# A Trainium2 transformer kernel without its filler products in four norms and the routing

## What is computed

```python
# first block, each layer l
h = rms_norm(x, g_norm_mix[l]) * (1 + sc1) + sh1
x = x + g1 * (concat(attention, hgrn2, gmlp of (h @ w_in[l])) @ w_out[l])
h = rms_norm(x, g_norm_ffn[l]) * (1 + sc2) + sh2
y = swiglu(h, ...)            # layer 0
y = moe_swiglu(h, ...)        # layer 1: 8 experts, the best 2 of each token
x = x + g2 * y
# then a norm by g_final, and the second block, each layer l
h = rms_norm_2(x, ln1_gain[l]);  x = x + concat(three mixers of (h @ w_in[l])) @ w_out[l]
h = rms_norm_2(x, ln2_gain[l]);  x = x + square(relu(h @ w_up[l])) @ w_down[l]
```

## Time and profile before

| | |
|---|---|
| median of 3 runs | 2403.26 us (2402.55 to 2404.16) |
| the profiled execution's own time | 2402.56 us |
| its span, first to last instruction | 2400.6 us |
| mean granted TensorE clock | 0.979 |
| TensorE busy with matmuls | 2308.3 us, 96% of the span |
| VectorE, ScalarE busy | 835.9 us (35%), 386.4 us (16%) |
| DMA | 582.92 MB, mean 243 GB/s |

### The profile page before, as it was taken

The page is one execution under the profiler, slowest core; times in us unless marked ns, Lnnn a source line. Parts: engine busy times, 40 slices in busy tenths (PEclk is TensorE's granted clock), DMA queues, the critical chain, the costliest instruction groups (busy, mean ns, idle before and its releaser), DMA issues.

```text
span 2400.6 us, 35155 instructions
## 1 busy us (share of the span) xinstructions
PE 2308.3 (96%) x15101; PEld 1612.3 (67%) x15102; DVE 835.9 (35%) x2042; ACT 386.4 (16%) x903; POOL 27.9 (1%) x52
## 2 busy tenths in 40 slices
PE   7999999999999999999999999899899999989999
PEld 5768888877764444434443444377589998659999
DVE  3663635048320000000000000144566742557663
ACT  3222100022320000000000000023521002441101
POOL 1010000000000000000000000000000000000000
PEclk9998999999899999999999999999999999999999
DMA  9473586622169999999989999973135463323441
GB/s 362 153 266 130 200 318 253 228 102 106 36 252 381 373 409 411 408 412 408 378 300 375 407 410 411 406 249 122 36 100 162 162 219 100 120 71 104 163 158 50
DMA packets 225518, 582.92 MB, mean 243 GB/s; under 512 B 19898, under 2 KB 79810, under 8 KB 213076
## 3 DMA queue, kind: packets, MB, share of 16 engines
q1 hardware_dynamic: 224788, 580.52, 64.6%
q0 software_dynamic: 576, 0.13, 0.0%
HBM read 579.58 MB, written 1.05 MB: 242 GB/s over the span
## 4 chain that ended last, share of the span: by engine, by line
PE 87%; DMA 4%; DVE 4%; SPq 2%; ACT 2%; issue 1%; DVEq 0%; ACTq 0%
PE wrk L2354 13%; PE acc L862 10%; PE wrk L1592 6%; PE acc L2414 5%; PE acc L3133 5%; PE acc L3165 5%; PE wrk L2339 4%; PE acc L865 4%; PE wrk L3165 4%; PE wrk L3133 4%; DMA ring<-in_moe_w_down_dram 3%; PE acc L1609 3%; PE wrk L2361 3%; PE acc L936 2%; PE acc L2397 2%; PE acc L951 2%
## 5 line engine op out<-in xcount | busy, mean ns | idle before, releaser
L2354 PE MATMUL wrk<-ring,hT 128*64 128x512 f32 (+1 forms) x1792 | 348.4, 542 | 6.6 <-DMA ring<-in_moe_w_up_dram 3.3
L2598 DVE TENSOR_TENSOR scratch<-scratch,wrk 128x512 f32<-128x512 f32 (+4 forms) x32 | 24.6, 768 | 802.5 <-PE wrk L2354 595.5
L862 PE MATMUL acc<-hT,ring 128*128 128x256 f32 (+2 forms) x1152 | 263.3, 385 | 1.3 <-ACT scratch L892 0.5
L2354 PEld LDWEIGHTS wrk<-ring,hT 128*64 128x64 f32 x1792 | 126.2, 137 | 204.1 <-issue 186.9
L862 PEld LDWEIGHTS acc<-hT,ring 128*128 128x128 f32 (+2 forms) x1152 | 211.3, 186 | 42.8 <-issue 4.4
L2414 PE MATMUL acc<-ring,scratch 128*64 128x512 f32 x784 | 177.7, 597 | 14.9 <-DMA ring<-in_moe_w_down_dram 14.9
L3210 DVE TENSOR_TENSOR ring<-ring 128x512 f32<-128x512 f32 (+1 forms) x192 | 155.2, 863 | 1.2
L1592 PE MATMUL wrk<-hT,ring 128*128 128x256 f32 x704 | 154.8, 380 | 0.0
L1592 PEld LDWEIGHTS wrk<-hT,ring 128*128 128x128 f32 x704 | 132.8, 190 | 18.6 <-ACT hT L748 0.9
L2414 PEld LDWEIGHTS acc<-ring,scratch 128*64 128x64 f32 x784 | 54.0, 136 | 116.9 <-issue 102.2
L3165 PE MATMUL acc<-scratch,ring 128*128 128x128 f32 x1024 | 117.6, 275 | 0.0
(11 more groups left out here) (439 smaller groups left out, 2713.2 us busy)
## 6 DMA issues: line engine op xcount, KB each, us to landing
ring<-in_moe_w_gate_dram SPq DMA_DIRECT2D x56, 2048.0 KB, 21.3
ring<-in_moe_w_up_dram SPq DMA_DIRECT2D x56, 2048.0 KB, 20.6
ring<-in_moe_w_down_dram SPq DMA_DIRECT2D x56, 2048.0 KB, 19.9
ring<-in_w_ada_dram SPq DMA_DIRECT2D x24, 2048.0 KB, 14.7
ring<-in_w_up_dram SPq DMA_DIRECT2D x32, 1024.0 KB, 7.4
ring<-in_w_down_dram SPq DMA_DIRECT2D x32, 1024.0 KB, 6.5
ring<-in_w_out_dram SPq DMA_DIRECT2D x8, 2048.0 KB, 8.1
ring<-in_w_in_dram SPq DMA_DIRECT2D x8, 1536.0 KB, 13.7
```

Of the source, the lines that this page charges most:

```text
L862: mm = pe.matmul(acc[p0:p0 + m, bank, 0:S], cols(k), hT[:, k, :], start=(k == 0), stop=(k == KD - 1))
L2354: mm = pe.matmul(flat_wrk[h * HD:h * HD + HD, lo:lo + n2], hT[:, k, 0:HD], w[:, at_, h * n2:(h + 1) * n2], start=(k == 0), stop=(k == KD - ...
```

## The change

The helper `keep_busy_pe` and its three calls go. Nothing else is altered.

```diff
@@ norm_pe
             if tag == ("mix", 1):
                 for i in range(4, 8):
                     ada_pe(pe, 1, i)
-            elif tag != ("mix", 0):
-                keep_busy_pe(pe, 10 if tag[0] == "ffn" else 7)
-
-        def keep_busy_pe(pe, n, bank=acc):
-
-            for _ in range(n):
-                pe.matmul(bank[:, 0, 0:S], ones, K("slot_ids"), start=True, stop=True)
@@ joint_norm_pe
                         mm.then_inc(pe_done, up("pe", "sum of squares", bank))
-            keep_busy_pe(pe, 7)
@@ route_pe
             mm.then_inc(pe_done, up("pe", "h turned"))
-            keep_busy_pe(pe, 6, wrk)
             pe.wait_ge(dve_done, at("dve", "selected"))
```

## The result

The changed kernel took 2421.32 us (median of 6 runs, 2417.67 to 2423.15), the kernel before in the same series 2407.59 us. The ratio is **1.0053**, with a 95% interval of 1.0039 to 1.0068: slower by 0.5%, where 0.5% was forecast. A second series of runs gave 1.0065 (1.0051 to 1.0078). The profiled execution took 2417.67 us, against 2402.56 for that of before. The kernel before itself ran anywhere from 2398 to 2414 us, so two single executions say little; the traces have to be taken apart.

The account below looks back on a forecast made before the run. PE, busy 96% of the span, was taken to bound the kernel. Three norms 4.5 plus routing 7.0 made 11.5 us on 2402.56, or 2414.1; 0.7 more for the median gave about 2415 us, range 2407 to 2421.

Parts of the forecast that it names:

- What bounds the kernel: Whole kernel: PE is busy 96% of the span, so time it loses in dense stretches is kernel time.
- What the removal takes off the path: All five filler places: other engines end the waits, so removal gains 0, at most 1 us.
- Norm 0: Layer 0's feed-forward norm: half clock in the dense products behind it costs 1.5 us, bounds 0 to 2.8.
- The two norms of the second block: First norms of both layers there: half clock in the dense work behind costs 1.5 us each, bounds 0 to 2.8.
- The term of 4.5 us for the three norms: Layer 0's feed-forward norm and the second block's two: 3 x 1.5 = 4.5 us, 0 to 8.4.
- The routing: Layer 1's feed-forward norm through the first gathering: thin work at half clock adds 7.0 us, 1 to 9.5.
- Rounds: Routing's 8 rounds of logits and transposes, 48 instructions: half clock adds 5.0 us.
- The sign that L2310 would start 6 to 7 us later: First gathering in the changed profile: starts 6 to 7 us later, measured from the norm's last square.
- That the rounds restore the clock: Rival in the routing: clock recovers after one low stretch; 7.5 us in all, 2411, chance 0.17.
- That the clock holds everywhere: Rival for all waits: clock never falls, not slower; 2402.3 to 2403.3 us, chance 0.10.
- Low for long: Rival: norms pay 2.5 us each, routing stays low until the experts, 9.5; 17 us, 2420, chance 0.12.
- The Trainium skill's rule on transposes: Routing's rounds: transposes do not count for the clock, so it stays low until the gathering; 14 us, 2417.

Follow-up runs that it names:

- no_layer1: Kernel before with the fillers left out only in layer 1's feed-forward norm and in the routing; ratio 1.0036.
- turns: Kernel before with each 256-column filler product replaced by four transposes of a 128 by 128 matrix; ratio 1.0009.
- no_norms: Kernel before with the fillers left out only in layer 0's feed-forward norm and the second block's two first norms; ratio 1.0021.
- pad26: Changed kernel plus 26 one-column products at the program's start, making its stream ahead of the second block as long as before; ratio 1.0046 to the kernel before.
- no_ffn1: Kernel before without only the ten fillers of layer 1's feed-forward norm, the routing's six kept; one run, 2409.12 us.
- half: Kernel before with about half of the fillers at each place, all at the start of the wait; ratio 1.0054.

## Why the prediction was right, and where not

**What bounds the kernel.** Right. Nothing behind the changed places took a delay up: from the end of the norm 0 column to layer 1's mixing norm 215.8 us passed in all fourteen executions, and the experts took 878 to 880.

**What the removal takes off the path.** Right, nothing: the first product in the norm of layer 0 started 0.16 us sooner after ScalarE's start, and with the clock held (norm 0 of no_layer1 and turns) the distance is 29.13 in either case.

**Norm 0.** 1.5 us forecast, 1.3 to 1.4 measured in all five executions without its fillers.

**The two norms of the second block.** 1.5 each forecast. Behind layer 1's it was 0, 1.7, 2.8 and 2.9 us in four executions, 1.8 on average; what follows the joint norm's wait cost 2.7 and 1.7 in the two profiles of the changed kernel and 2.9 in no_norms and pad26, 2.5 on average. The assumed stretch of 3.4 us was too short for these two: 6.8 us is as common. The term of 4.5 us for the three norms was undersized, at 1.4 + 2.5 + 1.8 = 5.7. The trace of the kernel before could have warned of it. The 4.18 us that the prediction reads the earlier trace rows are the busy part of a low stretch of 6.8 us, and with TensorE busy almost throughout one lasts four times 3.41 us, so that "the other low stretches read here last 3.41 us" comes from having read few (columns as in rows 11):

```profile
34.45:41.27 6.82, 4.17 (x7) 2.36 (x8) 1.75 (x10) 4.80 (x9) 0.00 (x0) 0.50 1.06 373
188.05:201.70 13.65, 12.87 (x132) 10.30 (x131) 6.57 (x13) 3.35 (x6) 0.00 (x0) 0.50 0.09 34
```

**The routing.** 7.0 us forecast, 6.1 measured. Rounds: 5.0 forecast; from the first logits to the counts it is 685.75 - 674.12 = 11.63 instead of 7.55 us, 4.1 more. Counts: 1.0 forecast; a pair every 0.43 instead of 0.22 us, 1.0. Gathering: 1.0 forecast, 6.56 - 5.41 = 1.15. The first term was too large because the first instructions still ran before the clock fell, and because a round then takes 1.17 / 0.62 = 1.9 times as long, not twice. The sign that L2310 would start 6 to 7 us later behind the norm's last square did not come: it is 4.9 us (19.37 against 14.43).

**The rivals.** That the rounds restore the clock is refuted by no_ffn1 (low to their end, 8.91 us) and by the 20.48 us of the changed kernel. That the clock holds everywhere is refuted by norm 0 and the routing of every kernel without fillers there; behind norm 1 it did hold once in four. "Low for long" came partly true for the second block's norms, but the routing never reached its upper bound. The Trainium skill's rule on transposes would have given 2417; turns shows that its reason does not hold in these waits.

**What the prediction did not have.** The sentence "the fillers wait for nothing and release nothing" led it to treat 40 products as free of any other effect. They also have a length in the instruction stream. Taking out 26 of them ahead of the second block moved its first norm in the stream, so that the exit from the experts took 1.1 to 1.7 us longer and a pause of 3.65 or 4.40 us fell into the squares. The clock fell there too, though hardly because of the pause: at 1578.98, ahead of it, in the first profile, and as it began (1585.61) in the second. In the first profile this is 1.65 us plus 6.3 us of longer squares (13.5 instead of 7.2). That part is nearly 8 us of the 18 at the five places, and it was not in any rival. That the measured 0.53% meets the forecast of 0.5% is so in part luck: by the columns the clock behind the waits costs 5.7 + 6.1 = 11.8 us, which pad26's 1.0046 (11.1 us) fits, and exit and pause come on top. In the medians that is 4.4 us in the first series (2421.3 against pad26's 2416.9) and 6.9 in the second; whether 2, 4 or 7 us of the whole belong to them the intervals do not settle. The time itself, 2421.3 where 2415 was forecast, is off by 6.5 us: 4.3 of them because the kernel before ran at 2407.6 in this series and not at the 2403.3 that the forecast started from, and 2.2 because the change cost 13.7 us and not 11.5.

## What to carry to other kernels

Fillers in a wait are there for what follows, so their price is read behind them: half the low stretch for dense work, and for thin work everything until dense work comes. What they are made of matters: in the norm of layer 0 and in the routing, one-column products or half the number were as bad as none, and transposes were as good as products. In the second block's norms half the number held the clock, so how few are enough has to be tried at each place. And whenever an edit changes the number of instructions ahead of a jump, compare the jump's length and look for pauses put down to "issue" behind it before the time is credited to the edit itself.

## What the runs showed of the hardware that was not expected

- Soon behind a jump, with the DMA engines full, TensorE stood still for 3.65, 4.40 and 4.59 us in three executions, and went on 1.3 to 1.5 us behind the end of a 16 KB packet of the instruction queue. The exit with the jump took anything from 3.65 to 7.40 us, and within 0.4 us the same wherever the number of instructions ahead was the same.
- Transposes of float32 kept the clock at 1.00 through waits of 4.4 and 3.0 us; one-column products, with PE counted busy for 4.25 of 4.25 us, did not in the norm ahead of the routing.
- Idleness of 1.83 us behind ten fillers was followed by a fall (half, norm of layer 0), while 2.09 us ahead of the joint norm was not the earlier trace rows, nor 3.71 us at the same place in no_layer1. The length of the idle time alone does not say whether the clock falls.
